# Attention probabilities divided by ScalarE in place and turned by plain transposes, in place of a matmul by scaled identities

## The reference

```
h = rms_norm(x);  proj = h @ w_in          # q, k, v of three kinds of attention, and gates
A: neighbourhood attention, 8 heads of 64, with a 2-D bias
B: three groups of 4 heads of 64 with dilated windows, merged by their softmax denominators
C: attention into 256 memory tokens, 4 heads of 128
merged = sum of sigmoid(gate) * (branch @ w_branch);  x = x + merged @ w_out
x = x + MoE(rms_norm(x))                    # 32 experts, top 4, clamped SwiGLU
out = rms_norm(x)
```

## Time and profile before

| | |
|---|---|
| median of 3 runs | 1239.45 us (1239.34 to 1240.58) |
| the profiled execution | 1241.22 us; its span is 1239.4 us |
| busy time over the span | PE 1182.7, PEld 611.0, DVE 269.3, ACT 255.8, POOL 207.3 us |
| moved by DMA | 456.40 MB, 368 GB/s over the span |
| chain that ended last | 59% PE, 37% DMA, 1% each of DVE, ACT and issue |

### The profile page before, as it was taken

One profiled execution on the slowest core, in us unless ns is written; L12 is line 12 of the kernel. 1 busy time (PEld: TensorE's weight loads), 2 busy tenths in 40 slices (PEclk: granted clock), 3 DMA queues, 4 the chain that ended last, 5 costly groups with the idle time before them and its releaser, 6 DMA issues.

```text
span 1239.4 us, 14318 instructions
## 1 busy us (share of the span) xinstructions
PE 1182.7 (95%) x6239; PEld 611.0 (49%) x6239; DVE 269.3 (22%) x539; ACT 255.8 (21%) x531; POOL 207.3 (17%) x89
## 2 busy tenths in 40 slices
PE   8999999999999999999999999999999989999996
PEld 8989877899533343333333333333333333333332
DVE  4147253232421111211111111121111111111112
ACT  6456455334310101101010010010001000000001
POOL 5865755687100000000000000000000000000000
PEclk9999999999999999999999999999999999999999
DMA  9754443499799999999999999999999999999995
GB/s 311 249 159 158 161 159 119 132 352 404 277 416 435 429 429 430 427 431 427 430 429 429 430 434 429 433 425 432 430 430 432 427 434 423 432 429 430 428 426 235
DMA packets 61255, 456.40 MB, mean 368 GB/s; under 512 B 5145, under 2 KB 33593, under 8 KB 43272
## 3 DMA queue, kind: packets, MB, share of 16 engines
q1 hardware_dynamic: 61192, 455.47, 89.3%
HBM read 454.39 MB, written 1.07 MB: 367 GB/s over the span
## 4 chain that ended last, share of the span: by engine, by line
PE 59%; DMA 37%; DVE 1%; ACT 1%; issue 1%; POOL 0%; SPq 0%; DVEq 0%; POOLq 0%; ACTq 0%
PE ps L540 58%; DMA arena<-in_expert_w_gate_up 33%; DMA arena<-in_expert_w_down 3%; PE ps L832 1%; DMA arena<-in_w_mem_kv 1%; ACT arena L1022 0%; POOL w_parts L529 0%; PE ps L826 0%; DVE x_normed L1468 0%; DVE neg_max L1308 0%; ACT w_parts_odd L1002 0%; PE ps L646 0%; PE ps L547 0%; PE ps L623 0%; DVE arena L1297 0%
## 5 line engine op out<-in xcount | busy, mean ns | idle before, releaser
L540 PE MATMUL ps<-arena,gathered_T 128*64 128x512 f32 x2048 | 473.7, 611 | 39.1 <-DMA arena<-in_expert_w_gate_up 39.1
L540 PE MATMUL ps<-arena 128*64 128x512 f32 (+6 forms) x1666 | 342.4, 537 | 2.8 <-DMA arena<-in_expert_w_down 1.3
L540 PEld LDWEIGHTS ps<-arena,gathered_T 128*64 128x64 f32 x2048 | 145.5, 140 | 307.3 <-issue 270.2
L540 PEld LDWEIGHTS ps<-arena 128*64 128x64 f32 (+3 forms) x1666 | 135.8, 154 | 199.4 <-issue 193.0
L529 POOL TENSOR_TENSOR w_parts<-arena,w_parts 128x1024 fp32r<-128x1024 f32 x42 | 102.9, 2472 | 50.5 <-ACT w_parts L1002 40.8
L529 POOL TENSOR_TENSOR w_parts_odd<-arena,w_parts_odd 128x1024 fp32r<-128x1024 f32 x38 | 90.9, 2413 | 49.4 <-ACT w_parts_odd L1002 49.4
L1412 DVE TENSOR_SCALAR arena<-arena 128x128 f32<-128x128 f32 x64 | 19.3, 343 | 317.8 <-PE ps L826 317.8
L1143 ACT COPY arena<-ps 128x256 f32<-128x256 f32 x32 | 11.9, 372 | 361.2 <-PE ps L826 361.2
L1418 DVE TENSOR_SCALAR arena<-ps 128x512 f32<-128x512 f32 x32 | 22.1, 691 | 274.4 <-PE ps L540 274.4
L1134 ACT ACTIVATE gathered_T<-ps,g_cols 128x128 f32<-128x128 f32 x128 | 36.5, 368 | 171.4 <-PE ps L540 171.4
L540 PEld LDWEIGHTS ps<-arena,x_normed 128*128 128x128 f32 x512 | 59.5, 191 | 24.8 <-issue 24.3
(11 more groups left out here) (178 smaller groups left out, 729.8 us busy)
## 6 DMA issues: line engine op xcount, KB each, us to landing
arena<-in_expert_w_gate_up SPq DMA_DIRECT2D x54, 4096.0 KB, 39.4
arena<-in_expert_w_down SPq DMA_DIRECT2D x62, 2048.0 KB, 39.7
arena<-in_expert_w_gate_up SPq DMA_DIRECT2D x20, 2048.0 KB, 13.0
arena<-in_w_in SPq DMA_DIRECT2D x29, 1024.0 KB, 5.3
arena<-in_w_out SPq DMA_DIRECT2D x4, 1024.0 KB, 11.5
arena<-in_expert_w_down SPq DMA_DIRECT2D x4, 1024.0 KB, 41.0
arena<-in_w_mem_kv SPq DMA_DIRECT2D x3, 1024.0 KB, 12.1
arena<-t_scratch SPq DMA_DIRECT2D x6, 384.0 KB, 3.7
```

Source lines behind the costliest of these rows:

```text
L540: return nc.tensor.matmul(out, lhsT, rhs, start=start, stop=stop, **kw)
```

## The change

`turn_probs` becomes eight transposes with the plain identity. A new function `divide(u)` on ScalarE multiplies the unit's four 128x256 tiles of exponentials by their reciprocal sums, in place, and signals `divided`, for which `turn_probs` waits. It stands in ScalarE's loop behind `high_part(i + 2)` and ahead of the move of chunk i's product, in the step in which the unit is turned. VectorE still takes the reciprocal, but makes no scaled identities; their memory is not used any more.

```diff
             def turn_probs(u):
-                o = OUTPUT_OF[u]
-                pe.wait_ge(scale_ready, o + 1)
+                pe.wait_ge(divided, u + 1)
...
-                            last = mm(ps[:, 6 + hh, kt * S + tt * P:kt * S + (tt + 1) * P],
-                                      scores[:, u % 4, hh, tt, kt * P:(kt + 1) * P], scaled_ident[:, o % 2, 2 * hh + tt, :],
-                                      True, True)
+                            last = nc.tensor.transpose(ps[:, 6 + hh, kt * S + tt * P:kt * S + (tt + 1) * P],
+                                                       scores[:, u % 4, hh, tt, kt * P:(kt + 1) * P], ident[:])
                 last.then_inc(probs_turned, 1)
...
+            def divide(u):
+                o = OUTPUT_OF[u]
+                act.wait_ge(inverse_ready, o + 1)
+                for hh in range(2):
+                    for tt in range(T):
+                        p = scores[:, u % 4, hh, tt, :]
+                        last = nc.scalar.mul(p, p, inv_sum[:, o, 2 * hh + tt:2 * hh + tt + 1])
+                last.then_inc(divided, 1)
...
                 if i - 1 in STEP_AFTER and STEP_AFTER[i - 1] in LAST_OF_B:
                     exps(STEP_AFTER[i - 1])
+                if i in STEP_AFTER and 0 <= STEP_AFTER[i] - TURN_LAG < NU:
+                    divide(STEP_AFTER[i] - TURN_LAG)
                 if i in WIDE_LAST:
                     act.wait_ge(chunk_used, i + 1)
                     move_wide(i, 1)
...
-                        link(vec.reciprocal(inv_sum[:, o, :], total))
-                        if o >= 2:
-                            dve.wait_ge(probs_turned, last_unit_of(o - 2) + 1)
-                        for c in range(4):
-                            last = vec.tensor_scalar(scaled_ident[:, o % 2, c, :], ident[:], inv_sum[:, o, c:c + 1], None, ALU.mult)
-                        last.then_inc(scale_ready, 1)
+                        vec.reciprocal(inv_sum[:, o, :], total).then_inc(inverse_ready, 1)
```

More of the change, by code:

```diff
@@ L243, in build @@
         mkT = area(FRONT0 + 14336, MEM_HEADS, MEM)
-        scaled_ident = area(FRONT0 + 15360, 2, 4, P)
         gates = area(FRONT0 + 16384, T, D)
@@ L335, in build @@
         scores_ready, scores_drained = sem("scores_ready"), sem("scores_drained")
-        max_ready, exp_done, scale_ready = sem("max_ready"), sem("exp_done"), sem("scale_ready")
+        max_ready, exp_done, inverse_ready, divided = sem("max_ready"), sem("exp_done"), sem("inverse_ready"), sem("divided")
         probs_turned, pT_dve, pT_act = sem("probs_turned"), sem("pT_dve"), sem("pT_act")
```

## The result

The changed kernel takes 1286.56 us (median of 6 runs, 1283.51 to 1287.76), the kernel before 1239.41 us (6 runs, 1239.27 to 1240.58). The ratio is 1.0371, with a 95% interval of 1.0361 to 1.0382: 47 us slower by the medians. The forecast was 1281 us, within 1265 to 1291.

A forecast was written before the change was run, and what follows sets the result against it. TensorE was taken to bound the front, and expert weight transfers the part from 611 us on. Waits net of shorter turns, +28.3 us, plus lost clock, +13.5, gave +41.8: 1281.3 us, range 1265 to 1291.

The forecast's parts named there:

- The front's shift reaches the end one to one: Expert weight transfers are issued behind events of the front, so any shift of the front passes unchanged to the end.
- The wait behind the casts: Front, twelve turns: TensorE waits for divisions queued behind ScalarE's casts; net of shorter turns, +28.3 us in all.
- the seven ordinary steps: Steps 4 to 8, 10 and 11: turn begins 2.76 us later and is 0.90 shorter, +1.86 us each, +13.0 together.
- step 3: Front: ScalarE is late with exponentials of unit 2; the turn starts 5.01 us later, less 0.90, +4.1 us.
- step 9: Front: TensorE waited for VectorE before; now the turn is 2.41 us later, less 0.90, +1.5 us.
- steps 12 to 14: Front turns without `head_scores`: 4.14 us late, less 0.90, +3.24 us each, +9.7 us for three.
- The shorter turn: Eight transposes take 0.88 us where the matmuls took 1.78: 0.90 us less in each of 12 turns, 10.8 in all.
- The clock: Front: TensorE drops to half clock behind nine of twelve waits, 1.5 us each, +13.5 us; bounds nothing to 20.3.
- The clock holds: Rival, chance 0.24: waits as forecast, but TensorE stays at full clock; +28.3 us, 1267.8 us.
- Faster: Rival, chance 0.04: divisions are ready before TensorE asks and the transposes give 10.8 us; 1228.7 us.
- ScalarE falls behind: Rival, chance 0.09: divisions delay ScalarE's moves and exponentials, some 2 us more in most steps; about 1300 us.
- the expert stream absorbs it: Rival, chance 0.03: DMA bounds the last 600 us regardless of the front, so a late front costs nothing; 1239 to 1245 us.

The follow-up runs named there:

- filled runs: Against the changed kernel, TensorE makes throwaway matmuls (one run) or transposes (the other) while it waits for the divisions: 1268.6 and 1268.5 us.
- the run with the divisions first: Against the changed kernel, the four divisions moved to the head of ScalarE's work for the chunk, ahead of the casts and their wait: 1234.2 us.
- the run with the late division and the matmul turn: Against the changed kernel, the turn is an fp32 matmul by the plain identity instead of transposes, the division still behind the casts: 1300.0 us.

## Why the prediction was right, point by point

- **The front's shift reaches the end one to one.** Right. The front grew by 46.0 us, the expert part by 1.0 us (917.8 to 918.8).
- **The wait behind the casts.** Right, in place and size: the turn of step 4 starts 3.81 us behind `head_scores` (3.82 worked out), idle time 2.68 us (2.7); four divisions take 1.70 us. The wait and the shorter turn together were put at +28.3 us; with the clock held, the run shows 29 us (1268.6 against 1239.8), and 26.9 and 27.2 in the profiled fronts of the two filled runs (327.9 and 328.2, less 301.0). Step by step, by the second of these, the seven ordinary steps cost 1.79 us each (1.86 worked out), step 3 4.05 (4.1), step 9 1.48 (1.5), steps 12 to 14 3.04 to 3.07 (3.24, since the row at 219.00 is a weight load that ran ahead; the first product of the turn stood at 219.23). The bound from below for the division, 1.57 us, was too low.
- **The shorter turn.** 0.88 us for eight transposes was right at full clock (0.86), and the 0.90 us gained per turn show as 8.6 to 9.9 us in place of 10.8 over twelve.
- **The clock.** The mechanism was right; its size was low. I took 9 losses at 1.5 us, 13.5 us. There were ten losses, three of them of about double length, and they cost 18 us. (The windows give some 21 us, seven times 1.7, and 3.4, 3.1 and 2.7; a part of that falls into the waits themselves.) This term holds most of what the forecast of 1281 fell short by. That a lost clock can last twice as long was in none of the rows of before. That the count came so near is in part luck: it was carried over from waits for transfers in another part of the kernel, and which waits lose the clock differs between kernels whose waits have the same lengths (steps 4 and 5). What makes the loss long in steps 3, 4 and 14, and why steps 6 and 9 lost none, stays open.
- **The clock holds** (0.24) was the price of a kernel that does not idle, not of this one: the filled runs gave 1268.5 where the rival said 1267.8.
- **Faster** needed divisions that start before the casts. That is the run with the divisions first, 1234.2 us; the order on ScalarE's queue decided the sign, as said.
- **ScalarE falls behind; the expert stream absorbs it.** Neither happened.

The weighed rule of the Trainium skill ("TensorE: Matmul & The Clock Gate", Part 4), that transposes don't hold the clock, did not hold for these fp32 transposes: 22 or 30 of them in each wait kept it at 1.00 and gave the same time as matmuls. The wait at 13.29 us, which I read as agreeing, then says nothing of transposes. The other advice ("ScalarE: Activation LUTs", Rules for kernel authors), to put multiplications on VectorE, was not what mattered: on ScalarE they cost little once they stand in the right place. No run divides on VectorE.

## What to carry to other kernels

When work is moved to an engine that is mostly idle, look at what stands ahead of it in that engine's queue, not at the engine's busy share: here 1.70 us of division, which costs next to nothing where it is well placed, became a wait of 2.7 us because 1.90 us of casts, which themselves waited for the consumer, stood ahead. Place such work ahead of the next wait for the consumer, or a step earlier. Where TensorE bounds a stage, price a wait of some 2 us or more above its length, for the clock: here 29 us of net waits cost 18 us more. The length alone does not say which wait will lose it (two of 1.79 us did, one of 3.04 us did not), so such a price is an average. Filling the waits with throwaway products, which is no cure, is a quick way to tell the wait from the clock.

## What the runs showed of the hardware

- fp32 transposes put into the twelve waits kept TensorE's granted clock at 1.00 from 90 to 290 us, as fp32 matmuls did (1268.5 and 1268.6 us).
- Six of the seven waits of 2.68 us in steps 4 to 8, 10 and 11 were followed by half clock in the changed kernel, five of the seven in the run with the late division and the matmul turn. In the run that divides ahead of the casts, the seven waits of 0.73 us were followed by none, two of 1.79 us by half clock, one of 1.80 and one of 3.04 us by none. The wait of 2.56 us in the run with the divisions first lost none either.
- Half clock behind a wait can last about twice as long as usual: 0.51 and 0.56 over 7 us behind the waits of 4.93 and 2.68 us in steps 3 and 4, against 0.76 in seven other steps.
